# Mixer into feed-forward on one core: the second x tile's norm goes ahead of a weight rest, and the last transposes go into the third block of products

## The reference, cut to what matters

```python
for i in range(DEPTH):                              # 4
    m = mixer_i(rms_norm(x, norm_gains[i, 0]))      # ends in "@ w_out"
    x = x + rms_norm(m, norm_gains[i, 1])
    f = swiglu(rms_norm(x, norm_gains[i, 2]), w_gate, w_up, w_down)
    x = x + rms_norm(f, norm_gains[i, 3])
```

## Time and profile before

| | us |
|---|---|
| median of 3 runs | 1480.89 (1480.83 to 1487.47) |
| the profiled execution: its time | 1474.92 |
| the profiled execution: its span | 1472.3 |
| TensorE busy in it | 1389.1 |
| VectorE busy | 1013.5 |
| ScalarE busy | 797.7 |

### The profile page before, as it was taken

The page is one execution under the profiler, slowest core; times in us unless marked ns, Lnnn a source line. Parts: engine busy times, 40 slices in busy tenths (PEclk is TensorE's granted clock), DMA queues, the critical chain, the costliest instruction groups (busy, mean ns, idle before and its releaser), DMA issues.

```text
span 1472.3 us, 20490 instructions
## 1 busy us (share of the span) xinstructions
PE 1389.1 (94%) x6849; PEld 1128.0 (77%) x6849; DVE 1013.5 (69%) x1962; ACT 797.7 (54%) x1560; POOL 156.9 (11%) x303
## 2 busy tenths in 40 slices
PE   6898899998999999998989999999989999899998
PEld 5687788887788788887868888777768888777556
DVE  4986755558645755569657555599768776679875
ACT  5564645455654654546646545457655545575434
POOL 3000000000110100002000000000029991000000
PEclk9999999999999999999999999999999999999999
DMA  7443466564432565654226555544346556443132
GB/s 243 152 149 108 137 221 198 173 198 150 151 115 86 187 213 174 196 173 138 90 79 208 192 179 192 180 156 144 115 136 209 190 171 199 143 143 116 57 116 85
DMA packets 154240, 230.49 MB, mean 157 GB/s; under 512 B 7496, under 2 KB 103056, under 8 KB 154176
## 3 DMA queue, kind: packets, MB, share of 16 engines
q1 hardware_dynamic: 152176, 224.18, 46.6%
q0 software_dynamic: 2000, 5.50, 1.4%
HBM read 228.60 MB, written 1.05 MB: 156 GB/s over the span
## 4 chain that ended last, share of the span: by engine, by line
PE 84%; DVE 11%; ACT 3%; issue 1%; POOL 0%; DMA 0%; DVEq 0%; ACTq 0%; POOLq 0%
PE ps L1954 24%; PE ps L1956 24%; PE ps L1955 24%; DVE w_rest L1272 2%; PE ps L2701 1%; DVE x L1333 1%; PE ps L1974 1%; PE ps L2158 1%; PE ps L2099 1%; PE ps L2601 1%; ACT w_head L757 1%; ACT scr_a L744 1%; DVE qkv L1379 1%; DVE xt_rest L1279 0%; DVE qkv L1377 0%
## 5 line engine op out<-in xcount | busy, mean ns | idle before, releaser
L1954 PE MATMUL ps<-w_head,xt_head 128*128 128x512 f32 (+1 forms) x1344 | 531.3, 395 | 20.1 <-DVE xt_rest L1279 8.1
L1956 PE MATMUL ps<-w_head,xt_rest 128*128 128x512 f32 (+1 forms) x1344 | 518.7, 386 | 0.0
L1955 PE MATMUL ps<-w_rest,xt_head 128*128 128x512 f32 (+1 forms) x1344 | 517.5, 385 | 0.0
L1272 DVE SCALAR_TENSOR_TENSOR w_rest<-w_raw,gain_t,w_head 128x512 fp32r<-128x512 f32 (+1 forms) x600 | 417.8, 760 | 78.0 <-ACT w_head L757 77.1
L757 ACT ACTIVATE w_head<-w_raw,gain_t 128x512 fp32r<-128x512 f32 (+1 forms) x600 | 373.9, 699 | 140.4 <-PE ps L1956 123.1
L1954 PEld LDWEIGHTS ps<-w_head,xt_head 128*128 128x128 f32 x1344 | 254.3, 189 | 75.1 <-issue 13.2
L1956 PEld LDWEIGHTS ps<-w_head,xt_rest 128*128 128x128 f32 x1344 | 253.9, 189 | 51.9
L1955 PEld LDWEIGHTS ps<-w_rest,xt_head 128*128 128x128 f32 x1344 | 254.7, 190 | 46.2
L1270 DVE TENSOR_TENSOR w_rest<-w_raw,w_head 128x1024 fp32r<-128x1024 f32 x124 | 150.0, 1251 | 87.8 <-ACT w_head L757 87.8
L757 ACT ACTIVATE w_head<-w_raw 128x1024 fp32r<-128x1024 f32 x124 | 124.5, 1054 | 104.2 <-PE ps L1956 93.8
L1954 PE MATMUL ps<-w_head,ht_head 128*128 128x512 f32 x352 | 137.4, 390 | 5.7 <-DVE ht_rest L1830 5.7
(11 more groups left out here) (455 smaller groups left out, 1384.5 us busy)
## 6 DMA issues: line engine op xcount, KB each, us to landing
w_raw<-in_ffn_w_gate_dram SPq DMA_DIRECT2D x88, 512.0 KB, 4.0
w_raw<-in_ffn_w_up_dram SPq DMA_DIRECT2D x88, 512.0 KB, 5.0
w_raw<-in_ffn_w_down_dram SPq DMA_DIRECT2D x88, 512.0 KB, 4.3
w_raw<-in_a_w_in_dram SPq DMA_DIRECT2D x48, 512.0 KB, 4.7
w_raw<-in_b_w_in_dram SPq DMA_DIRECT2D x24, 512.0 KB, 4.7
w_raw<-in_w_in_dram SPq DMA_DIRECT2D x24, 512.0 KB, 4.6
w_raw<-in_a_w_out_dram SPq DMA_DIRECT2D x16, 512.0 KB, 4.1
w_raw<-in_c_w_in_dram SPq DMA_DIRECT2D x10, 512.0 KB, 4.5
```

Of the source, the lines that this page charges most:

```text
L1272: ins = dve.scalar_tensor_tensor(w_rest[:, s, w], w_raw[:, s, w], by, hd, ALU.mult, ALU.subtract)
L1954: pe.matmul(out_, hd, wh, start=first, stop=False)
L1955: pe.matmul(out_, hd, wr, start=False, stop=False)
L1956: return pe.matmul(out_, rt, wh, start=False, stop=last)
```

## The change

It changes the order of work of VectorE and of TensorE in the four entries into a feed-forward. Nothing is added to the work or taken from it.

- VectorE: `rest(split - 1)` goes from in front of `mean_begun(1)`, `rsqrt_half(1)` and `entered(1, 0)` to behind them, and `xt_rest_of(2)` comes directly behind it, ahead of `posted(1, 1)` and `entered(1, 1)` instead of after them.
- TensorE: `transposes(3)` goes from in front of `products(2)` to its middle, between its second and its third quarter.
- Two hooks of `entry` that nothing used (`first`, `middle`) and the branch for `by_half` false around them are gone. The other entries, which are called without `late`, keep their order.

```diff
                 xt_rest_of(0, True)
                 xt_rest_of(1, True)
-                if late:
-                    rest(split - 1)
                 mean_begun(1, at[1, 0])
                 rsqrt_half(1, at[1, 1])
                 entered(1, 0)
+                if late:
+                    rest(split - 1)
+                    xt_rest_of(2, True)
                 posted(part[1, 1], at[1, 1], True)
                 dve.wait_ge(raw_done, n["add"] + 1)
                 entered(1, 1)
-                xt_rest_of(2, True)
+                if not late:
+                    xt_rest_of(2, True)
                 if not late:
                     rest(split)
                 xt_rest_of(3, True)
...
-            def entry(u, waits, by_half, first=lambda: None, second=1, between=lambda: None, middle=lambda: None, narrow=False):
+            def entry(u, waits, by_half, second=1, between=lambda: None, narrow=False, late=False):
...
-                def products(g):
+                def products(g, amid=None):
...
                         pe.wait_ge(rest_done, quarters(unit) + t + 1)
+                        if amid and t == 2:
+                            amid()
...
                 products(0)
-                if by_half:
-                    transposes(2)
-                    products(1)
+                transposes(2)
+                products(1)
+                if late:
+                    products(2, lambda: transposes(3))
                 else:
-                    middle()
-                    products(1)
-                    first()
-                    transposes(2)
-                transposes(3)
-                products(2)
+                    transposes(3)
+                    products(2)
                 products(3)
...
-                entry(u, xs(), True)
+                entry(u, xs(), True, late=True)
                 u = ffn(u)
```

## The result

| | before | changed |
|---|---|---|
| median of 6 executions, us | 1479.59 (1477.53 to 1487.47) | 1467.22 (1466.27 to 1468.44) |
| ratio to before, 95% interval | | 0.9918 (0.9894 to 0.9941) |
| the profiled execution: time, us | 1474.92 | 1466.51 |
| its span, us | 1472.3 | 1464.5 |

A forecast was written before the change was run, and what follows sets the result against it. TensorE, busy for 94% of the span, was taken as the bound, losing time where it has nothing to do. Four entries at 2.08 us gave 8.3 us, from 1480.89 to 1472.6 us; range 1468.5 to 1478.3.

The forecast's parts named there:

- The wait of 3.09 us: TensorE's wait for VectorE's x before transposes(2) in each feed-forward entry; forecast to fall to about 0.4 us.
- The new wait before products(1): TensorE would wait 0.27 us for the first quarter of w_rest, since VectorE's rest of unit u + 1 now starts later.
- Products(3) waits 0.2: TensorE would wait 0.18 us for the last xt_rest, with two quarters of products over the copy and subtraction instead of four.
- Transposes(3) wait for nothing in their new place: In the middle of products(2), x would be there 0.23 us before TensorE wants it; in the old place, 1.13 us wait.
- An entry gains 2.05 us: Each of the four feed-forward entries was forecast to gain 2.08 us on TensorE up to gate_up.
- the 0.76 kept for the range: Possible cost per entry of TensorE following VectorE quarter by quarter; taken as nothing; as a rival, time 1475.6, chance 0.14.
- The second feed-forward gives nothing back: After the entry, ScalarE and VectorE come 1.02 us sooner; the rest of unit u + 3 would be 0.97 us early.
- the load moved 2.6 us back: SyncE's load of unit u + 4, issued 2.58 us later, would cost nothing, with 8 us left over.
- the tables in the fourth entry: GpSimd builds tables beside VectorE's rests; ht_rest would be 0.09 us early, so no loss was taken from the 2.08.
- tables collide: Rival: VectorE's rests wait for GpSimd's table instructions, fourth entry gives nothing; gain 6.2 us, time 1474.7, chance 0.08.
- the step from the profiled execution to the median: The profiled execution lies 6.0 us below the median; the median would move by the same 8.3 us, to 1472.6.
- more than forecast: Rival: the new waits of 0.27 and 0.18 do not show, TensorE keeps 2.65 an entry; gain 10.6, time 1470.3, chance 0.07.

The follow-up runs named there:

- e2: VectorE's new order alone, TensorE in the order of the kernel before: 1466.56 us median of 6, ratio 0.9911 to the kernel before.
- e11: The changed kernel with ten matmuls of no use in the four waits left at each feed-forward entry: 1467.89 us, ratio 0.9898 to the kernel before.
- e5: The kernel before with 13 matmuls of no use in the 3.09 us wait of each feed-forward entry: 1474.09 us median of 12, ratio 0.9953.
- e10: The kernel before with 3, 3, 2 and 13 matmuls of no use in TensorE's waits at each feed-forward entry: 1477.14 us, ratio 0.9953.
- e13: The changed kernel with TensorE's waits filled in the four entries into a feed-forward and the three into a mixer: 1468.26 us, ratio 0.9923 to before.
- e14: VectorE's new order alone, TensorE's waits filled in the four feed-forward and three mixer entries: 1470.09 us, ratio 0.9938 to the kernel before.
- e1: The kernel before, unchanged, timed against itself: 1482.2 us median of 12, ratio 1.0016.
- e3: TensorE's new order alone, VectorE in the order of the kernel before: 1482.11 us median of 12, ratio 1.0018 to the kernel before.
- e8: The changed kernel again, in the second comparison on another chip: 1466.4 us, ratio 0.9918 to the kernel before.

## Why the prediction was wrong, point by point

**Right, by its own steps.** The wait of 3.09 us falls to 0.42 (forecast: about 0.4). The new wait before products(1) is 0.34 (0.27). Products(3) waits 0.2 (0.18). Transposes(3) wait for nothing in their new place. An entry gains 2.05 us (2.08). TensorE follows VectorE's quarters at no cost: products(1) and the first half of products(2), 18 matmuls, take 482.57 - 478.38 = 4.19, 0.23 each, so the 0.76 kept for the range does not show. The second feed-forward gives nothing back, nor does the fourth at its first hidden chunk; the load moved 2.6 us back costs nothing. The split by parts, 1.25 for VectorE's alone, is in e2's stretches.

**Partly wrong: the tables in the fourth entry.** The prediction checked the first hidden chunk and took no loss. The second one loses 0.6 us wherever a fall has not already taken it, except in e11. The rival "tables collide" had this mechanism, at a price of 2.08 us instead of 0.6; the sign it gave for such a wait was one within 20 us of the entry, and it came at 44. It makes the gain smaller, so it is no part of the miss.

**Wrong: the step from the profiled execution to the median.** The prediction says that "nothing in the change bears on why executions differ, so the median moves by as much". The profiled execution of before had no fall in its entries; its falls lay at 117 and 1431 us and in the first 60. The 6.0 us between it and the median was noted and put at nothing in the gain, though much of it was a term that the change removes. The runs: filling the long wait takes 5.0 us from the kernel before (e5), and filling the short ones too 6.9 us (e10), with the order unchanged. The order gives 7.9 us (e10 against e11). The whole was 12.4 us in the comparison that decided the result and 16.2 of span in the third (1481.1 - 1464.9), where the sum of the parts is 14.8; with intervals as wide as 8.7 to 15.7 us these agree. The kernel before varied from 1478.8 to 1484.0 us by median over the four comparisons, the changed one from 1466.4 to 1468.6. The range went wrong with the same step: it held 1.8 us for scatter at its low end. How much each execution of before lost to falls in its entries is not known, since only two of them were traced, of 1472.3 and 1474.5 us of span; that many do is inferred from the two fillings, their mean clocks and the 2.8 us of the traced fall.

The rival "more than forecast" (the new waits do not show) named the right side and the wrong mechanism: the new waits are there. None of the rivals had the clock.

**What stays open.** TensorE's part of the change shortens the stretches by 2.7 us (774.7 against 771.9) and does not show in the time: 30 executions of the changed kernel have a mean of 1467.7 us at a mean clock of 0.9922, 18 of VectorE's order alone 1467.6 at 0.9936. The lower clock is measured. That a fall at an entry costs 0.6 us in the one and none in the other is seen in e2's and the changed kernel's rows. The mixers are where 2.7 us can get lost: in the unfilled profiles they sum to 491.8 to 495.1 us in the changed kernel (five profiles) and 489.6 to 495.0 in VectorE's order alone (three), and four of the five changed ones have a fall at 340 us, in the second mixer, that none of the three has. These are too few to show that this is the whole of it. Why the clock falls more often with the transposes in the middle is not known, nor what picks the places where it falls; e13 and e14 point the same way, but their 1.8 us rest on six executions each.

## What to carry to other kernels

A wait of TensorE can cost more than its length: price it by its row, and then ask what the clock did behind it in executions other than the profiled one. When a profiled execution lies some us off the median, the gap belongs to the working of the sum; look up the granted clocks of the single executions before calling it scatter. Then look for where the clock fell, since one fall cost nothing, 0.6 or 2.8 us here, depending on its place. A quick test for the clock's share is to fill the wait with work of no use: if the kernel gets faster with its order unchanged, the wait was costing clock. Filling can also cost, where it takes away a wait that hid a fall (e5) or holds back what it stands in front of (e13).

## What the runs showed of the hardware that was not expected

- The granted clock is at 1.00 or 0.50 (2.4 or 1.2 GHz) and between only in windows in which a fall begins or ends; a fall covers 3 to 4 us (1080 to 1085 in the changed kernel), or over 6 us where it comes behind the 3.07 us wait (771 to 777 in e1). It came after waits of 0.65, 0.73 and 0.54 us in a row as well as after one of 3 us, and in one execution but not in another of the same kernel. The page "TensorE: Matmul & The Clock Gate" of the Trainium skill, section "The HAM clock gate", has two levels that go with how busy the array was, 1.2 and 2.4 GHz. The trace agrees with the two levels.
- 13 extra matmuls in each of four waits make the kernel before 5.0 us faster (e5), with 8 more in the short waits of each entry 6.8 us (e10).
- The same fall costs 0 us where a wait of TensorE follows it (194.31 against 194.30), 0.6 at an entry of the changed kernel, 1.3 under products(0) of e5, 2.8 at the end of the 3.07 us wait, and 1.4 to 1.5 near the end of the fourth mixer.
- The table work of GpSimd stretches VectorE's four rests to 2.99 us in the changed kernel, 3.29 before and 3.87 in e3, against 2.74 alone, depending on how much of it they meet; at most 1.13 us for the four, so not each of them is held up by a whole instruction of 0.84. The two rests of the next down unit, of 128x1024 each, take 4.30 us in e8 against 2.35 before.
